# Delta-rule inverse: products, copies and updates on the half of the columns that a level couples

## The reference, cut to what matters

```python
lmat = jnp.where(strict, jnp.einsum('rnid,rnjd->rnij', kb, k) * decay, 0.0)
amat = jnp.eye(c, dtype=jnp.float32) + lmat
rhs = jnp.concatenate([v * beta[..., None], kb * jnp.exp(gcum)[..., None]], axis=-1)
sol = lax.linalg.triangular_solve(amat, rhs, left_side=True, lower=True, unit_diagonal=True)
u, w = sol[..., :dv], sol[..., dv:]
```

## Time and profile before

| what | value |
|---|---|
| median of 3 executions | 3001.21 us (3001.19 to 3001.32) |
| profiled execution, its own time | 3017.27 us |
| its span, first to last instruction | 3015.5 us |
| mean granted clock of TensorE in it | 0.911 |
| delta stage, L831 to L921 | 177.6 to 319.6 us |
| the 28 steps of the inverse | 217.1 to 294.1 us |
| busy in these 77.0 us: PE, PEld, DVE, ACT, POOL | 76.91, 76.74, 36.64, 16.73, 33.08 us |

### The profile page before, as it was taken

The page is one execution under the profiler, slowest core; times in us unless marked ns, Lnnn a source line. Parts: engine busy times, 40 slices in busy tenths (PEclk is TensorE's granted clock), DMA queues, the critical chain, the costliest instruction groups (busy, mean ns, idle before and its releaser), DMA issues. The chain is left out here.

```text
span 3015.5 us, 27217 instructions
## 1 busy us (share of the span) xinstructions
PE 2353.4 (78%) x10328; PEld 1611.9 (53%) x10328; DVE 1819.8 (60%) x2497; ACT 824.0 (27%) x1050; POOL 468.8 (16%) x402
## 2 busy tenths in 40 slices
PE   3969798778977877777766596899994946599995
PEld 2649686555222222222245583677773844378774
DVE  3455652544925555555574264688885575488885
ACT  1121101101010000000010131577761040277774
POOL 0003000000023334344301000111101031001110
PEclk9989899889989999999987797899996977699998
DMA  4420251334789999999923103799984500489995
GB/s 148 169 84 1 70 195 48 140 107 163 275 335 421 422 422 421 421 421 421 420 85 100 42 1 114 253 386 383 386 334 161 189 0 4 160 332 399 399 385 220
DMA packets 235349, 711.37 MB, mean 236 GB/s; under 512 B 20407, under 2 KB 24847, under 8 KB 202291
## 3 DMA queue, kind: packets, MB, share of 16 engines
q1 hardware_dynamic: 185268, 394.91, 36.5%
q0 software_dynamic: 48960, 312.50, 25.3%
q10 hardware_dynamic: 992, 2.23, 0.2%
HBM read 686.45 MB, written 23.14 MB: 235 GB/s over the span
## 5 line engine op out<-in xcount | busy, mean ns | idle before, releaser
L1498 PE MATMUL psum<-experts_uv_rows,experts_weight_diagonal 128*128 128x512 f32 x1024 | 509.2, 621 | 149.6 <-DVE experts_weight_diagonal L1508 149.6
L131 DVE TENSOR_TENSOR moe_weight_parts<-weight_ring,moe_weight_parts 128x2048 fp32r<-128x2048 f32 x228 | 512.2, 2288 | 105.5 <-ACT moe_weight_parts L2178 105.5
L1513 DVE SCALAR_TENSOR_TENSOR experts_uv_rows<-experts_uv_rows,peer_x 128x1024 f32<-128x1024 f32 x256 | 313.9, 1226 | 292.6 <-DMA experts_uv_rows<-peer_uv,experts 292.6
L2178 ACT ACTIVATE moe_weight_parts<-weight_ring 128x2048 fp32r<-128x2048 f32 x228 | 423.6, 1908 | 113.9 <-DMA weight_ring<-moe_w 112.7
L1498 PEld LDWEIGHTS psum<-experts_uv_rows,experts_weight_diagonal 128*128 128x128 f32 x1024 | 174.9, 190 | 484.1 <-DVE experts_weight_diagonal L1508 359.6
L1483 POOL DMA_INDIRECT experts_uv_rows<-peer_uv,experts x256 | 257.1, 1004 | 584.2 <-PE psum L1498 357.6
L137 PE MATMUL psum<-moe_weight_parts,moe_block_x_parts 128*128 128x512 f32 x608 | 245.7, 404 | 29.1 <-DVE moe_weight_parts L131 24.2
L139 PE MATMUL psum<-moe_weight_parts,moe_block_x_parts 128*128 128x512 f32 x608 | 239.9, 395 | 0.0
L138 PE MATMUL psum<-moe_weight_parts,moe_block_x_parts 128*128 128x512 f32 x608 | 239.9, 395 | 0.0
L1490 ACT ACTIVATE experts_gelu<-experts_dots 128x1 f32<-128x1 f32 x256 | 51.9, 203 | 596.4 <-DVE experts_uv_rows L1513 596.4
L137 PE MATMUL psum<-project_x_parts,project_weight_parts 128*128 128x256 f32 x544 | 161.5, 297 | 46.5 <-DVE project_weight_parts L131 46.5
(11 more groups left out here) (513 smaller groups left out, 3769.4 us busy)
## 6 DMA issues: line engine op xcount, KB each, us to landing
weight_ring<-moe_w SPq DMA_DIRECT2D x114, 2048.0 KB, 11.9
weight_ring<-ada_w SPq DMA_DIRECT2D x24, 2048.0 KB, 8.0
weight_ring<-w_in SPq DMA_DIRECT2D x17, 2048.0 KB, 8.5
moe_results<-moe_block_out POOLq DMA_DIRECT2D x38, 512.0 KB, 6.9
weight_ring<-hgrn_w_in SPq DMA_DIRECT2D x8, 2048.0 KB, 9.0
weight_ring<-nsa_w_in SPq DMA_DIRECT2D x5, 2048.0 KB, 7.8
weight_ring<-peer_wq SPq DMA_DIRECT2D x4, 2048.0 KB, 8.2
weight_ring<-w_out SPq DMA_DIRECT2D x2, 2048.0 KB, 7.7
```

The costliest lines, as they stand in the source:

```text
L131: return eng.tensor_tensor(out.bitcast(F32R), x, high, ALU.subtract)
L1498: last = nc.tensor.matmul(S.ps[:, 2 * a + c, :], diag[:, t % 4, :], uv[:, t % BUFS, 1, c * BANK:(c + 1) * BANK], start=(i == 0), stop=(i = ...
L1513: nc.vector.scalar_tensor_tensor(uv[:, t % BUFS, 0, :], uv[:, t % BUFS, 0, :], 1.0, x2[:, a, :], ALU.mult, ALU.mult, accum_out=dots[:, t:t ...
L2178: act.activation(half(m, h)[:, 0, :].bitcast(F32R), raw_half(m, h), ACT.Copy).then_inc(high_made, 1)
```

## The change

- The order of `GROUPS` becomes (0,0), (1,0), (0,1), (1,1), so that consecutive steps alternate in direction. `FIRST` stays indices 0 and 3; `SECOND` becomes indices 2 and 1 (before 1 and 2).
- A view `halves(m, level, second)` names, for each head, the 64 of the 128 columns that lie in the first or second block of every pair: single columns with a gap of one at level 0, runs of 2 with gaps of 2 at level 1, up to one run of 64 at level 6.
- The 4 products of `first` and the 8 of `second` have 64 moving and 64 output columns in place of 128. Their stationary operands stay 128 x 128.
- ScalarE copies 4 x 64 columns, and VectorE's two subtractions work on 4 x 64 columns.
- The stationary `pr` of the last four products must be zero outside its half. So the copy goes to a tile `products` with a place of its own for each level and direction (128 x 7168 float32), which GpSimd sets to zero once at the start of the stage. ScalarE waits for that before its first copy of the loop (semaphore `cleared`).
- Masks, GpSimd's operations of each step, the number of instructions on every engine in the loop and all other waits stay as they are.

```diff
--- before.py
+++ after.py
@@ -746,7 +746,7 @@
 
 
     nc = S.nc
-    GROUPS = [(r, a) for r in range(2) for a in range(NT)]
+    GROUPS = [(r, a) for a in range(NT) for r in range(2)]
     FIRST = [GROUPS.index((0, 0)), GROUPS.index((1, 1))]
     SECOND = [GROUPS.index((0, 1)), GROUPS.index((1, 0))]
     with Stage(S, "delta") as st:
@@ -772,10 +772,11 @@
         tt = st.sb("inverse_t", [P, 4, NH, P])
         mk = st.sb("masked", [P, 2, NH, P])
         pr = st.sb("product", [P, 2, NH, P])
+        products = st.sb("level_products", [P, LEVELS, 2, NH, P])
         names = ("in_ab", "chain", "act_chain", "g_ready", "gcum_made", "gcum_copied", "rows_made", "rows_read",
                  "grams_made", "grams_read", "turned", "turned_read", "masked", "prod_made", "prod_read", "upd_made",
                  "upd_read", "rhs_ready", "u_made", "u_read", "s_made", "s_read", "w_made", "w_read", "o_made", "softplus",
-                 "sig", "state_rows", "pool_chain", "sigb", "gexp", "g_rows")
+                 "sig", "state_rows", "pool_chain", "sigb", "gexp", "g_rows", "cleared")
         s = {n: st.sem(n) for n in names}
         up, lo = S.cst[:, C_UP:C_UP + P], S.cst[:, C_LO:C_LO + P]
         one = [P, NH, P]
@@ -785,6 +786,9 @@
             return c.rearrange("p (h o) -> p h o", o=1).to_broadcast(one)
         def bank(b):
             return S.ps[:, b, :].rearrange("p (h t) -> p h t", h=NH)
+        def halves(m, level, second):
+
+            return m.rearrange("p h (j s b) -> p s h j b", s=2, b=1 << level)[:, second]
 
         with nc.Block() as block:
             @block.sync
@@ -822,7 +826,10 @@
                     act.wait_ge(s["prod_made"], n + 1)
                     if n >= 2:
                         act.wait_ge(s["upd_made"], n - 1)
-                    act.activation(pr[:, n % 2, :, :], bank(n % 2), ACT.Copy).then_inc(s["prod_read"], 1)
+                    if n == 0:
+                        act.wait_ge(s["cleared"], 1)
+                    level, r = n // 4, GROUPS[n % 4][0]
+                    act.activation(halves(products[:, level, r], level, r), halves(bank(n % 2), level, r), ACT.Copy).then_inc(s["prod_read"], 1)
 
             @block.vector
             def _(dve):
@@ -886,8 +893,9 @@
                         i = 4 * level + n
                         dve.wait_ge(s["upd_made"], i + 1)
                         b = 2 + 2 * (i % 2)
-                        nc.vector.tensor_tensor(tm[:, n, :, :], tm[:, n, :, :], bank(b), ALU.subtract).then_inc(s["upd_read"], 1)
-                        nc.vector.tensor_tensor(tt[:, n, :, :], tt[:, n, :, :], bank(b + 1), ALU.subtract).then_inc(s["upd_read"], 1)
+                        here, turned_here = halves(tm[:, n], level, r), halves(tt[:, n], level, 1 - r)
+                        nc.vector.tensor_tensor(here, here, halves(bank(b), level, r), ALU.subtract).then_inc(s["upd_read"], 1)
+                        nc.vector.tensor_tensor(turned_here, turned_here, halves(bank(b + 1), level, 1 - r), ALU.subtract).then_inc(s["upd_read"], 1)
 
 
 
@@ -922,7 +930,7 @@
 
             @block.gpsimd
             def _(pool):
-
+                nc.gpsimd.memset(products[:, :, :, :, :], 0.0).then_inc(s["cleared"], 1)
                 for level in range(LEVELS):
                     for n, (r, a) in enumerate(GROUPS):
                         pool.wait_ge(s["grams_read"], n + 1)
@@ -976,8 +984,10 @@
                     pe.wait_ge(s["upd_read"], 2 * i + 2)
                     if i >= 2:
                         pe.wait_ge(s["prod_read"], i - 1)
+                    level, r = i // 4, GROUPS[n][0]
+                    out, inverse = halves(bank(i % 2), level, r), halves(tm[:, n], level, r)
                     for h in range(NH):
-                        last = mm(bank(i % 2)[:, h, :], mk[:, i % 2, h, :], tm[:, n, h, :])
+                        last = mm(out[:, h], mk[:, i % 2, h, :], inverse[:, h])
                     last.then_inc(s["prod_made"], 1)
 
                 def second(i):
@@ -986,10 +996,13 @@
                     pe.wait_ge(s["prod_read"], i + 1)
                     if i >= 2:
                         pe.wait_ge(s["upd_read"], 8 + 2 * (i - 1))
+                    level, r = i // 4, GROUPS[n][0]
+                    out, product = halves(bank(b), level, r), halves(products[:, level, r], level, r)
                     for h in range(NH):
-                        mm(bank(b)[:, h, :], tt[:, n, h, :], pr[:, i % 2, h, :])
+                        mm(out[:, h], tt[:, n, h, :], product[:, h])
+                    out, inverse = halves(bank(b + 1), level, 1 - r), halves(tt[:, n], level, 1 - r)
                     for h in range(NH):
-                        last = mm(bank(b + 1)[:, h, :], pr[:, i % 2, h, :], tt[:, n, h, :])
+                        last = mm(out[:, h], products[:, level, r, h, :], inverse[:, h])
                     last.then_inc(s["upd_made"], 1)
                 for i in range(4 * LEVELS + 1):
                     if i < 4 * LEVELS:
```

## The result

The changed kernel takes **3076.78 us** (median of 4 runs, 3073.46 to 3080.01) where the kernel before, run beside it on the same chip, takes 3001.27 (4 runs, 3001.19 to 3009.4): ratio 1.0245, with the interval 1.0223 to 1.0266. It is slower, by the mechanism that the prediction named, and 1.8 us beyond the upper end of its range. One of the 23 executions of the kernel before that stand beside runs e5 to e8 took 3694.89 us at a mean granted clock of 0.637, in a slower state of the chip, and enters no ratio.

The account below looks back on a forecast made before the run. PE, with its 128 x 128 weight loads, was taken to bound the inverse loop. Terms 0 + 66.1 - 0.5 + 0 + 0.2 gave +66 us on 3001.21: 3067 us, own range 3063 to 3072, full range 2998 to 3075.

Parts of the forecast that it names:

- What bounds the kernel: Inverse loop: PE sets the pace at 112 ns per matmul instruction, the 128 x 128 load taking about as long as streaming.
- Part 1, the products: The loop's 672 load and matmul pairs: still 112 ns each at an unchanged clock with half the stream, so 0.
- the two bounds: Limits on the products' time: 38 us less if streaming alone counted, 21 us more if gapped PSUM writes slowed levels 0 and 1.
- Part 2, the clock: Inverse loop: granted clock stays at 0.50 for all 28 steps, 213 ns per instruction, 143.1 us in all, +66.1 us.
- the clock is high after all: Rival for the loop: 64 columns suffice or the clock does not drop at the start; 2999 to 3002 us, chance 0.18.
- the change leaves that idle time alone, so the clock falls again: Before the loop: PE still idles from 215.2 to 217.2, so the clock falls to 0.50 with the first steps.
- The rival in which 64 columns bring the clock back on the way: Loop: low level lasts for only part of levels 0 and 1, 3019 us, or up to 3045 if later; chance 0.11.
- Part 3, copies and updates: ScalarE's copies and VectorE's updates shrink but stay hidden in idle time; only the last two subtractions save, -0.5 us.
- Part 4, the memset: GpSimd zeroes the products tile at stage start in 6.1 us, done by about 184; ScalarE's new wait costs 0.
- Part 5, the order: Before the loop: ScalarE waits for the third group first, then copies twice in a row; +0.2 us (0 to 0.6).
- Behind the loop: The 16 products after the loop take 3.4 us at the low level instead of 2.02, covered by VectorE; 0, at most +1.5.
- I take the difference as constant: Final sum: the profiled execution stands 16 us above the unprofiled median, before and after, giving 3001.21 + 66 = 3067 us.

Follow-up runs that it names:

- e5: The changed kernel with only the first of the three products of each step back to 128 moving columns; 3005.2 us, ratio 0.9994 to the kernel before.
- e8: The kernel before, with level 0's second products left out and its first product and masked operand subtracted directly from the identity; 3004.97 us, ratio 0.9993.
- e3: The changed kernel plus ten unread products of 128 columns in PE's idle time ahead of the loop; 3007.67 us, ratio 0.9998 to the kernel before.
- e6: e3 with the loop's stationary matrices cut from 128 to 64 columns, read for time only; 2969.73 us, ratio 0.9883 to the kernel before.
- e1: The changed kernel run once more, beside the kernel before on the chip of the later runs; 3074.73 us, ratio 1.0228.
- e2: The changed kernel with all products back to 128 moving and output columns, the rest of the change kept; 3004.62 us, ratio 0.9999 to the kernel before.
- e9: e7 with the first product of each step at 128 columns; 3013.16 us, ratio 1.0026 to the kernel before.
- e7: e3 plus eight extra ScalarE copies before its copy of step 12, so PE idles once mid-loop; 3044.82 us, ratio 1.0133 to the kernel before.
- e10: e8 plus four mask buffers, four banks at level 0 and eight unread products ahead of level 1; 2999.49 us, ratio 0.9978 to the kernel before.

## Why the prediction was right, and where its sum was off

**What bounds the kernel: right.** PE alone releases the other engines, before and after (the three lines of waits).

**Part 1, the products: right, 0.** The reading of rows 4, that 20 columns behind a load of 128 take what 128 take, holds for 64: e3 shows 112 ns at the high level, the changed kernel 213 at the low one, and e6 shows that the stationary side is what stands there. Neither of the two bounds is touched. Writing PSUM with gaps cost nothing: 2.68 us a step at level 0 in e3. The prediction had taken levels 0 and 1 alone to be in question, without a row for it; no level shows a cost. The Trainium skill (PSUM — Partial Sum Buffer, table row "Cachelines") says that any non-contiguous pattern slows matmuls significantly; at 64 columns no run shows it, neither behind a load of 128 columns nor in e6 behind one of 64, where eight instructions of level 0 (from 219.88 to 220.34) go at 58 ns each. What shorter loads would uncover stays open.

**Part 2, the clock: right in mechanism and nearly in size.** +66.1 us was predicted; from the first to the last product the loop takes 76.9 us before (217.16 to 294.07) and 141.7 after (216.78 to 358.47), **+64.8**. The 1.3 us between them have a place. I had the low level from the very first step, as in rows 7; in the changed kernel the first 16 instructions still ran high, in 1.97 us (row at 216.78) where 213 ns each make 3.4, and those of the kernel before took 3.46:

```profile
217.16 3.46 PE L938 MATMUL psum<-delta_inverse,delta_masked 128*128 128x128 f32 x16 [2.00 <-DVE delta_inverse_t L882]
```

The rival "the clock is high after all" had its reason half right: 64 columns do hold the high level (e3). It failed on the other half, the start, as argued against it. But the step "the change leaves that idle time alone, so the clock falls again" rested on one profile and was in part luck. With about 2 us of idle time ahead of the loop in each, the clock fell in the traces of before, of the changed kernel and of e1, and did not fall in those of e2 and e5, whose products are wider. All 8 executions of the changed kernel took 3072 to 3080 us, so it fell in all of them, and in the two traces it fell only after 2 us of gapless 64-column products. So the narrow products may share in the fall itself, and not only fail to undo it; no run tells the two apart. Where the fall is taken away (e3), or a third of the products is wide (e5, and e9 with its pause), the kernel lands at or near that rival's price. The rival in which 64 columns bring the clock back on the way is refuted by the windows of 300 to 358 and by e7. That rows 6 speak against reading "busy" as PE's busy time holds as well: PE is busy 58.00 of 58.00 us at 0.50.

**Part 3, copies and updates: right.** They are hidden (4.37 us of idle time a step). At the tail, from the last L897 to the first L905 it is 359.17 - 358.50 = 0.67 us; before it was 1.20. That is -0.53, and -0.5 was predicted.

**Part 4, the memset: right.** 6.07 us for 6.1, over at 178.8 for "by about 184", and ScalarE's first copy is released by PE.

**Part 5, the order: the release right, the 0.2 us not seen.** VectorE's L861 is now released by ScalarE and not by PE as in rows 10: the pair ends at 190.22, VectorE starts at 190.35. Counted from the stage's first operation (176.47, before 177.57) that is 13.88 us, where it was 13.99. The loop itself starts 0.7 us later in the stage (40.31 us in for 39.59): the difference arises in the Gram part, where VectorE waits for PE at the low clock (0.38 us ahead of 202.75, for instance; before it did not wait there). The part behind the loop is 0.7 us shorter, 0.5 of it part 3. So the stage's sum equals the loop's only because these two cancel.

**Behind the loop: right.** The 16 products take 3.75 us where 3.4 was said, and end at 363.75, while VectorE works up to 365.19.

**The sum is where it missed.** Over the whole stage the traces give 142.9 us before and 207.7 after, +64.8, and +65.3 in e1, where 66 was predicted. The median moved by 75.5 in the first comparison and by 66.5 in e1's. The failed step is the last one of the prediction, "I take the difference as constant": 16 us between the profiled execution of before (3017.27) and the median of its 3 runs. The changed kernel's profiled execution, 3073.46, is no slower than its other runs, and the later runs of the kernel before that enter the ratios lie between 2995.76 and 3022.47. So 3017.27 was one draw from that scatter and not an offset, and 3001.21, the median of 3 runs within 0.13 us, was a low base, which three runs so close to each other did not show: the medians of the later 23 to 25 runs are 3005.74 to 3008.24, 4.5 to 7 us higher. With the stage at its predicted size, that makes most of the distance between 3067 and 3076.78; the rest is of the size of the scatter. What makes the runs scatter by 20 us, and whether the chips differ, was not looked into.

**What stays open.** That 64 columns alone never bring the clock back is seen in this loop only. What decides whether the clock falls at the start is open too: it fell before and after the change and in e1, not in e2 and e5, with about the same idle time.

## What to carry to other kernels

This is what this loop suggests. Before narrowing the moving side of float32 matmuls, find a row with the same stationary size and few moving columns: if its starts are as far apart as now, the load is the bound, and there is nothing to gain but on the stationary side. Then look at the granted clock where the stream begins: a narrowed stream can hold the high level and yet not win it back, so one idle time ahead of it can double the time of all that follows, as it did here. A few wider products, in the stream (e5, e9) or in the idle time ahead of it (e3), cost nothing that could be measured here, and a span measured once is no offset to a median.

## What the runs showed of the hardware that was not expected

**VectorE beside GpSimd.** In e10 the same VectorE operation, 512 elements with both inputs in SBUF, takes 0.68 us or twice as long. Timeline of e10:

```profile
218.37 0.68 DVE L883 TENSOR_TENSOR delta_inverse_t<-constants,delta_masked 128x512 f32<-128x512 f32 x1
...
219.22 1.28 POOL L936 TENSOR_TENSOR delta_masked<-delta_lmat,constants 128x512 f32<-128x512 f32 x1 [1.37 <-DVE delta_inverse_t L883]
219.56 1.48 DVE L883 TENSOR_TENSOR delta_inverse_t<-constants,delta_masked 128x512 f32<-128x512 f32 x1
...
221.22 1.27 POOL L936 TENSOR_TENSOR delta_masked<-delta_lmat,constants 128x512 f32<-128x512 f32 x1 [0.72 <-DVE delta_inverse_t L883]
221.57 1.47 DVE L883 TENSOR_TENSOR delta_inverse_t<-constants,delta_masked 128x512 f32<-128x512 f32 x1
222.96 0.68 DVE L882 TENSOR_TENSOR delta_inverse<-constants,psum 128x512 f32<-128x512 f32 x1
```

At 218.37 no mask of GpSimd is running and it takes 0.68. At 219.56 and 221.57 it starts within a mask and ends about 0.55 us behind the mask's end (221.04 against 220.50; 223.04 against 222.49), as if it did most of its work only then. In e8 it takes 1.47 beside a mask as well (at 218.17), and 0.69 alone. L882, with one input from PSUM, takes 0.67 to 0.69 throughout, also at 218.97 and 220.97, where 0.4 us of it lie beside a mask. The Trainium skill (GPSIMD Engine Reference, table row "SBUF interfaces") says that GpSimd shares its SBUF interfaces with VectorE, with contention for instructions with two SBUF inputs; the rows agree and give it a size here, 0.8 us on 0.68.
